# Low weight parts of the convolution stage by an adding DMA instead of VectorE

## The chip, the cores and the metric

The kernel runs on one core of a Trainium2 chip. The metric is the device time of one execution in microseconds (us). Before the change three runs took 1458.36, 1458.60 and 1459.15 us; the median is 1458.6 us. Five engines work beside each other and are tied by semaphores: TensorE (PE in the rows; PEld is its weight load), VectorE (DVE), ScalarE (ACT), GpSimd (POOL) and SyncE (SP), which only issues DMAs here.

## The reference, cut to what matters

Two transformer blocks on 512 tokens of 1024 features, float32. The part around the change is the mixer of the second block:

```
def conformer_conv(x, w_in, b_in, conv_w, conv_b, ln_g, ln_b, w_out, b_out):
    a, g = jnp.split(x @ w_in + b_in, 2, axis=-1)
    h = a * jax.nn.sigmoid(g)
    h = lax.conv_general_dilated(h, conv_w[:, None, :], window_strides=(1,),
        padding=[(CONV_KERNEL - 1, 0)], ..., feature_group_count=D_MODEL) + conv_b
    h = jax.nn.silu(layer_norm(h, ln_g, ln_b))
    return h @ w_out + b_out
```

`CONV_KERNEL` is 31: every feature is convolved over time with its own 31 taps. `x @ w_in` is 1024 to 2048 features, `h @ w_out` 1024 to 1024.

## The kernel before, in words

**Dense layers.** Every weight matrix is cut into units of 128 output features (128 partitions x 1024 float32, 512 KB). A unit passes through four stages, in four slots (`SLOTS`): SP loads it into `raw`; ScalarE copies it to `whi`, which rounds it to the type float32r (`split_hi`, L891, semaphore `hi_done`); VectorE subtracts, `wlo = raw - whi` (`split_lo`, L1273, semaphore `lo_done`); TensorE multiplies eight tiles, three products for each (`whi*xh`, `whi*xl`, `wlo*xh`, L543 to L545). One unit is a chain of 24 matmuls into one PSUM bank. SP waits for `lo_done` of the unit that used the slot before; ScalarE waits for `chain_done` of that unit.

**The convolution stage.** It works on eight chunks c = 0 to 7 of 128 features. Chunk c needs two units of `w_ain`, 2c (gate) and 2c+1 (value). TensorE runs, for each c, the chains of units 2c and 2c+1, then `convolve(c-1)`, then `statistics(c-3)`. The 31 taps of a chunk are divided among the engines by three tables:

- `PE_TAPS`: taps on TensorE, as matmuls with diagonal weights, two taps to a pair (L817); ScalarE makes the diagonals (L1176).
- `POOL_TAPS`: ScalarE multiplies (`tapped`, L1190, a ring of 9 buffers), GpSimd adds (L532). n taps are n - 1 additions.
- `LATE_TAPS`: VectorE, after `convolve`, in the same PSUM bank (L1632).
- What is left are VectorE's own taps (L1619, L1622). A chunk that has some needs one more addition in `collect` (L1640).

The order on each engine is written out by hand. VectorE in chunk c: evict and gate the value unit (L1653, L1663, which gives `hc`), then own taps of c and late taps of c - 1 in turn, with the two `split_lo` of units 2c+3 and 2c+4 and the eviction of unit 2c+2 at fixed places among them, then `collect(c-1)` (L1640, L1645). ScalarE in chunk c: products, then `split_hi` of unit 2c+5, the sigmoid of the next chunk, the diagonals, `split_hi` of unit 2c+6. GpSimd in chunk c only adds. `hc` is copied in shifted form to `shifted` by four DMAs before `convolve` may start. Units 16 to 23 in this count are those of `w_aout`, of which TensorE begins three at once after the layer norm.

Of the kernel before, what the change touches and what calls it, by code (L numbers as in the profile page):

```python
# [22 lines left out]
F32 = mybir.dt.float32  # L23
F32R = mybir.dt.float32r
ALU = mybir.AluOpType
# [6 lines left out]
C = D // P  # L32
# [7 lines left out]
FF_PARTS = (8, 8, 6)  # L40
MLP_PARTS = (8, 8, 8, 8)
TAPS = 31
PE_TAPS = (8, 6, 6, 8, 8, 8, 14, 22)
SHIFTS = 2
GROUP = P // SHIFTS
GATE_AT = 8
DIAGS = 3
POOL_TAPS = (11, 11, 11, 11, 11, 10, 9, 5)
LATE_TAPS = (0, 6, 10, 12, 12, 13, 8, 0)
LATE_START = (2, 2, 2, 0, 0, 0, 0, 4)  # L50
PARTS = 9
LAST_DIAGS = 5
HC = 3
SLOTS = 4
AHEAD = 3
WARM = 10
# [104 lines left out]
def build(nc, xT, vec_in, cst_in, w_in, out):  # L161
# [3 lines left out]
    with ExitStack() as ctx:  # L165
# [76 lines left out]
        w_loaded = [sem(f"w_loaded{s}") for s in range(SLOTS)]  # L242
        hi_done = sem("hi_done")
        lo_done = sem("lo_done")
        chain_done = sem("chain_done")
        acc_free = sem("acc_free")
        setup = sem("setup")
# [130 lines left out]
        def used(unit):  # L378

            return 2 * unit + 2 if isinstance(unit, int) and unit < 4 else unit + 5  # L380

        def loads(base, i, k):

            return 16 * (i + (base + k) // SLOTS + 1)

# [4 lines left out]
        def _(sp):  # L390

            def load(p, i, k):
                unit = p.unit + SLOTS * i + k
                if isinstance(unit, int) and unit < SLOTS:
                    free, at = None, unit - p.unit
                elif isinstance(i, int):
                    free, at = unit - SLOTS + 1, SLOTS * i + k
                else:
                    free, at = sp.snap(unit - SLOTS + 1), sp.snap(SLOTS * i + k)
                if p.name == "ain":  # L400
                    at = at ^ 1
                src = p.weights[at] if isinstance(at, int) else \
                    p.weights[bass.ds(at, 1)].rearrange("o p n -> p (o n)")
                if free is not None:
                    sp.wait_ge(lo_done, free)
                sp.dma_start(raw[:, k, 0:p.tiles * P], src).then_inc(w_loaded[k], 16)

# [69 lines left out]
        @block.gpsimd  # L477
        def _(pool):


            pool.wait_ge(setup, 1)
            pool.wait_ge(cst_loaded, 16)
            for g in range(2):
                pool.wait_ge(squared, 2 * g + 2)
                nc.gpsimd.tensor_tensor(square_of(2 * g), square_of(2 * g), square_of(2 * g + 1), ALU.add)\
                    .then_inc(early_summed, 1)
            pool.wait_ge(early_summed, 2)
            nc.gpsimd.tensor_tensor(square_of(0), square_of(0), square_of(2), ALU.add).then_inc(early_summed, 1)
            nc.gpsimd.tensor_copy(near[:, 0, PAD:PAD + P], ident).then_inc(near_steps, 1)
            for g in range(4):  # L490
                pool.wait_ge(near_steps, g + 2)
                nc.gpsimd.tensor_tensor(near[:, g + 1, on], near[:, g, on],
                                        near[:, g, PAD - (1 << g):2 * PAD + P - (1 << g)], ALU.add)\
                    .then_inc(near_steps, 1)

            def add_squares(name):

                per = 2 if name == "ain" else 1
                for n in range(per * C):
                    which = n % 2 if name == "ain" else 0  # L500
                    x = (prod if name == "ain" and n // 2 % 2 else sq)[:, n % 2, :]
                    pool.wait_ge(sq_ready, SQ[name] + n + 1)
                    pool.wait_ge(ssum_ready, SS[name] + n + 1)
                    nc.gpsimd.tensor_tensor(ssum[:, which, :], ssum[:, which, :], x, ALU.add)\  # L504
                        .then_inc(ssum_ready, 1)

            add_squares("ffn0")
            add_squares("qkv")
            for s in range(len(STEPS)):
                k0 = P if STEPS[s][1] == 0 else 0  # L510
                pool.wait_ge(den_steps, 2 * s + 2)
                a = prob[:, s % 3, :, k0:2 * P]
                nc.gpsimd.tensor_tensor(a, a, stat[:, 5, s, :].rearrange("p (i o) -> p i o", o=1)
                                        .broadcast_to([P, REP, 2 * P - k0]), ALU.mult).then_inc(p_scaled, 1)
            for m in range(2 * C):
                at = slice(m // C * 2 * P, (m // C + 1) * 2 * P)
                pool.wait_ge(sq_ready, SQ["ffn1"] + m + 1)
                pool.wait_ge(ssum_ready, SS["ffn1"] + m + 1)
                nc.gpsimd.tensor_tensor(ssum[:, 0, at], ssum[:, 0, at], sq[:, m % 2, at], ALU.add)\
                    .then_inc(ssum_ready, 1)  # L520
            add_squares("ain")

            made = adds = 0
            for c in range(C):
                if c >= 2:
                    pool.wait_ge(hv_ready, c - 1)
                for k in range(1, POOL_TAPS[c]):
                    a = tapped[:, made % PARTS, :] if k == 1 else prod[:, c % 2, :]
                    pool.wait_ge(tapped_ready, made + k + 1)
                    if k > 1:  # L530
                        pool.wait_ge(tapped_steps, adds)
                    nc.gpsimd.tensor_tensor(prod[:, c % 2, :], a, tapped[:, (made + k) % PARTS, :], ALU.add)\  # L532
                        .then_inc(tapped_steps, 1)
                    adds += 1
                made += POOL_TAPS[c]
            add_squares("mlp")
# [3 lines left out]
        def _(pe):  # L540
# [6 lines left out]
            def chain(p, i, k, hi, lo):  # L547

                chain_no = p.chain + SLOTS * i + k
                pe.wait_ge(lo_done, p.unit + SLOTS * i + k + 1)  # L550
                pe.wait_ge(acc_free, chain_no - 3)
                for t in range(p.tiles):
                    w = slice(t * P, (t + 1) * P)
# [4 lines left out]
            def first_chains(name, norm_name, n=2):  # L558

                p = ph[name]  # L560
                pe.wait_ge(lo_done, p.unit + n)
                pe.wait_ge(acc_free, p.chain + n - 4)
                for t in range(C):
                    if t == C - 2 and norm_name != "ffn0":
# [298 lines left out]
                                          start=True, stop=True)  # L863
                mm.then_inc(spread_done, 1)
            fill(LN_FILL[2])
            pe.wait_ge(lo_done, p.unit + LN_UNITS)
            for t in range(C):
                pe.wait_ge(ln_lo, t + 1)
                w = slice(t * P, (t + 1) * P)
# [12 lines left out]
        def _(act):  # L882
# [309 lines left out]
                                         bias=v("conv_b", c) if k == 0 else 0.0).then_inc(tapped_ready, 1)  # L1192

            nc.scalar.activation(eps[:, 3:4], eps[:, 0:1], ACT.Sqrt)
            def square(c):

                act.wait_ge(hv_ready, c + 1)
# [19 lines left out]
            for c in range(C):  # L1217
# [12 lines left out]
                if c < C - 1:  # L1230
                    if c < C - 2:
                        split_hi(p.unit, 0, 2 * c + 2 + AHEAD)
                        sigmoid(c + 1)
                    if c + 1 == C - 1:
                        diagonals(c + 1, 1, 2)
                    else:
                        diagonals(c + 1)
                    if c < C - 2:
                        split_hi(p.unit, 0, 2 * c + 3 + AHEAD)
                else:  # L1240
                    split_hi(p.unit, 0, 2 * c + AHEAD)
                    split_hi(p.unit, 0, 2 * c + 1 + AHEAD)
# [21 lines left out]
        def _(dve):  # L1264
# [402 lines left out]
            for c in range(C):  # L1667
# [21 lines left out]
                gate_at = next((n for n in range(rounds) if issued[n] >= GATE_AT), rounds - 1)  # L1689
                for n in range(rounds):  # L1690
                    for j in range(2):
                        if n == split_at[j] and c < C - 1 and (c or j):
                            split_lo(p.unit, 0, 2 * c + j + AHEAD)
                    if n == gate_at and c < C - 1:
                        evict(c + 1, 0)
# [138 lines left out]
```

## Time and profile before

| | before |
|---|---|
| median of 3 runs | 1458.6 us |
| profiled execution, its own time | 1457.93 us |
| its span, first to last instruction | 1456.1 us |
| PE, PEld busy | 1442.8, 1174.9 us |
| DVE, ACT, POOL busy | 929.2, 631.2, 210.9 us |
| granted TensorE clock, mean | 1.00 of full speed (2.4 GHz) |

The profile was taken from one execution, whose own time stands beside its span: 1.8 us lie outside the span. Times in the rows count from the span's start. The convolution stage runs from about 914 us (first matmul of unit 0) to about 1049 us (last statistics). A busy PE is not PE at its peak, since matmuls overlap: starts of neighbouring matmuls are more telling than busy time.

### The profile page before, as it was taken

How to read it: one execution, taken by the hardware profiler on the slowest of the kernel's cores; microseconds unless marked ns; L12 is line 12 of the kernel's file. 1: busy time of each engine (PE TensorE's matmuls, PEld its weight loads, DVE VectorE, ACT ScalarE, POOL GpSimd, SP SyncE). 2: the span in 40 equal slices, each digit the busy share in tenths (PEclk: the TensorE clock that was granted, in tenths of full speed). 3: DMA queues.
4: the chain of work that ended last, by engine and by line, in shares of the span. 5: the costliest groups of instructions: out<-in, count | busy, mean ns of one | idle time of the engine just before them, and what ended most of it. 6: DMA issues, size and time to landing. Idle time of an engine off the chain costs nothing.

```text
span 1456.1 us, 19997 instructions
## 1 busy us (share of the span) xinstructions
PE 1442.8 (99%) x6852; PEld 1174.9 (81%) x6852; DVE 929.2 (64%) x1330; ACT 631.2 (43%) x999; POOL 210.9 (14%) x155
## 2 busy tenths in 40 slices
PE   9999999999999999999999999999999999999999
PEld 8788888888877898888888888766578888888887
DVE  7877773573645667767754756899998653544532
ACT  7444442342546665444432425777754322222210
POOL 4000000000302241000000004599611000000000
PEclk9999999999999999999999999999999999999999
DMA  5233233232422012332332333243313333232321
GB/s 191 86 101 101 88 103 113 78 104 81 131 81 69 30 60 87 101 102 87 101 116 72 102 96 92 87 130 88 102 33 105 111 102 99 90 104 95 102 94 50
DMA packets 42397, 137.01 MB, mean 94 GB/s; under 512 B 4960, under 2 KB 5984, under 8 KB 42336
## 3 DMA queue, kind: packets, MB, share of 16 engines
q1 hardware_dynamic: 41200, 133.80, 28.5%
q10 hardware_dynamic: 1136, 2.42, 0.4%
q8 instruction: 35, 0.57, 0.2%
q14 instruction: 26, 0.21, 0.0%
HBM read 129.85 MB, written 2.10 MB: 91 GB/s over the span
## 4 chain that ended last, share of the span: by engine, by line
PE 85%; POOL 7%; DVE 4%; ACT 2%; issue 1%; DMA 0%; ACTq 0%; POOLq 0%; DVEq 0%
PE bank L543 27%; PE bank L545 27%; PE bank L544 27%; POOL prod L532 6%; PE bank L691 1%; PE bank L719 1%; PE bank L704 1%; DVE bank L1622 1%; DMA cst<-cst_in 0%; DVE wlo L1273 0%; PE bank L584 0%; DVE hv L1746 0%; ACT res L1025 0%; DVE ylo L1712 0%; ACT whi L891 0%
## 5 line engine op out<-in xcount | busy, mean ns | idle before, releaser
L543 PE MATMUL bank<-xh,whi 128*128 128x512 f32 x1184 | 465.2, 393 | 1.5 <-DVE res L1561 0.7
L545 PE MATMUL bank<-xh,wlo 128*128 128x512 f32 x1184 | 461.2, 390 | 0.0
L544 PE MATMUL bank<-xl,whi 128*128 128x512 f32 x1184 | 461.0, 389 | 0.0
L891 ACT ACTIVATE whi<-raw 128x1024 fp32r<-128x1024 f32 x244 | 255.6, 1050 | 235.1 <-PE bank L545 233.8
L1273 DVE TENSOR_TENSOR wlo<-raw,whi 128x1024 fp32r<-128x1024 f32 x244 | 312.4, 1281 | 43.6 <-ACT whi L891 35.5
L543 PEld LDWEIGHTS bank<-xh,whi 128*128 128x128 f32 x1184 | 222.3, 188 | 55.8 <-issue 7.1
L544 PEld LDWEIGHTS bank<-xl,whi 128*128 128x128 f32 x1184 | 222.4, 188 | 46.7 <-issue 1.2
L545 PEld LDWEIGHTS bank<-xh,wlo 128*128 128x128 f32 x1184 | 222.3, 188 | 46.6
L543 PE MATMUL bank<-ahi,whi 128*128 128x512 f32 x608 | 236.7, 389 | 0.0
L544 PE MATMUL bank<-alo,whi 128*128 128x512 f32 x608 | 236.7, 389 | 0.0
L545 PE MATMUL bank<-ahi,wlo 128*128 128x512 f32 x608 | 236.6, 389 | 0.0
L1294 DVE TENSOR_TENSOR res<-bank,res 128x512 f32 (+1 forms) x80 | 55.2, 690 | 202.6 <-PE bank L545 202.6
L504 POOL TENSOR_TENSOR ssum<-ssum,sq 128x512 f32<-128x512 f32 x32 | 47.8, 1494 | 738.6 <-ACT sq L911 407.0
L1345 DVE SCALAR_TENSOR_TENSOR tmp<-u,vec,tmp 128x512 f32<-128x512 f32 x176 | 124.2, 747 | 31.8 <-ACT tmp L950 31.8
L544 PEld LDWEIGHTS bank<-alo,whi 128*128 128x128 f32 x608 | 114.2, 188 | 23.7
L545 PEld LDWEIGHTS bank<-ahi,wlo 128*128 128x128 f32 x608 | 114.2, 188 | 23.7
L543 PEld LDWEIGHTS bank<-ahi,whi 128*128 128x128 f32 x608 | 114.2, 188 | 23.6
L950 ACT ACTIVATE tmp<-u,vec 128x512 f32<-128x512 f32 x88 | 71.6, 814 | 125.3 <-DVE u L1340 125.3
L1340 DVE TENSOR_TENSOR u<-bank,rinv 128x512 f32<-128x512 f32 x88 | 59.4, 685 | 63.9 <-PE bank L545 63.9
L532 POOL TENSOR_TENSOR prod<-prod,tapped 128x512 f32<-128x512 f32 x63 | 92.9, 1475 | 9.3 <-POOL prod L532 0.4
L972 ACT ACTIVATE ahi<-tmp 128x512 f32 (+1 forms) x32 | 20.2, 632 | 121.8 <-DVE tmp L1370 121.8
L954 ACT ACTIVATE gate<-tmp 128x512 f32<-128x512 f32 x44 | 27.9, 633 | 96.2 <-DVE tmp L1345 96.2
(183 smaller groups left out, 1315.6 us busy)
## 6 DMA issues: line engine op xcount, KB each, us to landing
raw<-w_ffn_up SPq DMA_DIRECT2D x88, 512.0 KB, 3.4
raw<-w_ffn_down SPq DMA_DIRECT2D x32, 512.0 KB, 3.4
raw<-w_mlp_up SPq DMA_DIRECT2D x32, 512.0 KB, 3.3
raw<-w_mlp_down SPq DMA_DIRECT2D x32, 512.0 KB, 3.3
raw<-w_ain SPq DMA_DIRECT2D x16, 512.0 KB, 3.3
raw<-w_ffn_down SPq DMA_DIRECT2D x16, 384.0 KB, 3.1
raw<-w_qkv SPq DMA_DIRECT2D x12, 512.0 KB, 3.4
raw<-w_wo SPq DMA_DIRECT2D x8, 512.0 KB, 3.5
```

Source lines behind the costliest of these rows:

```text
L504: nc.gpsimd.tensor_tensor(ssum[:, which, :], ssum[:, which, :], x, ALU.add)\
L532: nc.gpsimd.tensor_tensor(prod[:, c % 2, :], a, tapped[:, (made + k) % PARTS, :], ALU.add)\
L543: nc.tensor.matmul(out_, hi, mh, start=first, stop=False)
L544: nc.tensor.matmul(out_, hi, ml, start=False, stop=False)
L545: return nc.tensor.matmul(out_, lo, mh, start=False, stop=last)
L891: nc.scalar.activation(whi[:, s, 0:tiles * P], raw[:, s, 0:tiles * P], ACT.Copy)\
L950: nc.scalar.activation(tmp[:, k, :], u[:, k, 2:2 + T], ACT.Identity, scale=col(vec, par + 2), bias=col(vec, par + 3))\
L954: nc.scalar.activation(gate[:, b, :], tmp[:, 2 * b + 1, :], ACT.Silu)\
L1273: V.tensor_tensor(wlo[:, s, 0:tiles * P], raw[:, s, 0:tiles * P], whi[:, s, 0:tiles * P].bitcast(F32), ALU.subtract).then_inc(lo_done, 1)
L1294: V.tensor_tensor(row(res, c), acc[k][:], row(res, c), ALU.add).then_inc(acc_free, 1)
L1340: V.tensor_tensor(u[:, k, 2:2 + T], acc[k][:], rinv[:], ALU.mult).then_inc(acc_free, 1)
L1345: V.scalar_tensor_tensor(tmp[:, k, :], u[:, k, shift:shift + T], col(vec, par + 4 * j + shift), tmp[:, k, :], op0=ALU.mult, op1=ALU.add).t ...
```

## The change

For units 5 to 16 of the stage (`ADDED`; 11 of `w_ain`, one of `w_aout`) the low part is made in another way. ScalarE writes `wlo = -whi` (`negate_high`), GpSimd then issues a DMA that reads the same weights from HBM again and adds them into `wlo`. GpSimd issues the two DMAs of units 2c+3 and 2c+4 ahead of its additions of chunk c. TensorE waits for that DMA (`low_added`) where it waited for `lo_done`; SP may refill `raw` as soon as `hi_done` is reached. VectorE's subtractions for these units go.

The tap tables change: TensorE has two taps fewer in chunks 3 and 4; GpSimd's additions go from 10, 10, 10, 10, 10, 9, 8, 4 to 10, 9, 8, 8, 8, 8, 7, 4; late taps are 60 instead of 61; VectorE's own taps go from 12, 8, 4, 0, 0, 0, 0, 4 to 12, 10, 7, 4, 3, 2, 0, 4, so that chunks 3, 4 and 5 need the additional `L1640`.

```diff
-PE_TAPS = (8, 6, 6, 8, 8, 8, 14, 22)
+PE_TAPS = (8, 6, 6, 6, 6, 8, 14, 22)
-POOL_TAPS = (11, 11, 11, 11, 11, 10, 9, 5)
-LATE_TAPS = (0, 6, 10, 12, 12, 13, 8, 0)
+POOL_TAPS = (11, 10, 9, 9, 9, 9, 8, 5)
+LATE_TAPS = (0, 5, 9, 12, 13, 12, 9, 0)
+ADDED = tuple(range(5, 17))
...
+        def low_parts(unit):
+
+            if isinstance(unit, int):
+                return unit + 1 - sum(ph["ain"].unit + e <= unit for e in ADDED)
+            return unit + 1
...
+        def wait_low(eng, unit, passed=0):
+
+            if is_added(unit):
+                eng.wait_ge(low_added[unit % SLOTS], 16 * added_in_slot(unit))
+            else:
+                eng.wait_ge(lo_done, low_parts(unit) - (0 if isinstance(unit, int) else passed))
...
-                if free is not None:
+                if is_added(unit - SLOTS):
+                    sp.wait_ge(hi_done, unit - SLOTS + 1)
+                elif free is not None:
                     sp.wait_ge(lo_done, free)
...
             for c in range(C):
+                for e in (2 * c + AHEAD, 2 * c + AHEAD + 1):
+                    if e in ADDED:
+                        pool.wait_ge(low_negated, ADDED.index(e) + 1)
+                        weights = ph["ain"].weights[e ^ 1] if e < 2 * C else ph["aout"].weights[e - 2 * C]
+                        nc.gpsimd.dma_start(wlo[:, e % SLOTS, :], weights, accum_op=ALU.add)\
+                            .then_inc(low_added[e % SLOTS], 16)
                 if c >= 2:
                     pool.wait_ge(hv_ready, c - 1)
...
             def chain(p, i, k, hi, lo):
 
                 chain_no = p.chain + SLOTS * i + k
-                pe.wait_ge(lo_done, p.unit + SLOTS * i + k + 1)
+                wait_low(pe, p.unit + SLOTS * i + k, passed(p))
...
+            def negate_high(e):
+
+                act.wait_ge(hi_done, p.unit + e + 1)
+                nc.scalar.activation(wlo[:, e % SLOTS, :], whi[:, e % SLOTS, :].bitcast(F32), ACT.Copy, scale=-1.0)\
+                    .then_inc(low_negated, 1)
+
...
                     if c < C - 2:
                         split_hi(p.unit, 0, 2 * c + 2 + AHEAD)
                         sigmoid(c + 1)
+                        negate_high(2 * c + 2 + AHEAD)
...
                     if c < C - 2:
                         split_hi(p.unit, 0, 2 * c + 3 + AHEAD)
+                        negate_high(2 * c + 3 + AHEAD)
...
-                        if n == split_at[j] and c < C - 1 and (c or j):
+                        if n == split_at[j] and c == 0 and j:
                             split_lo(p.unit, 0, 2 * c + j + AHEAD)
```

GpSimd, from its additions of chunk 0 on, before (L532 is an addition, `x9` nine alike; one pair of rows is one chunk):

```order
L532 TENSOR_TENSOR prod<-tapped 128x512
L532 TENSOR_TENSOR prod<-prod,tapped 128x512 x9
L532 TENSOR_TENSOR prod<-tapped 128x512
L532 TENSOR_TENSOR prod<-prod,tapped 128x512 x9
L532 TENSOR_TENSOR prod<-tapped 128x512
L532 TENSOR_TENSOR prod<-prod,tapped 128x512 x9
```

The same place after the change (L568 is the addition, L559 the adding DMA):

```order
L568 TENSOR_TENSOR prod<-tapped 128x512
L568 TENSOR_TENSOR prod<-prod,tapped 128x512 x9
L559 DMA wlo<-w_ain 128x1024 x2
L568 TENSOR_TENSOR prod<-tapped 128x512
L568 TENSOR_TENSOR prod<-prod,tapped 128x512 x8
L559 DMA wlo<-w_ain 128x1024 x2
L568 TENSOR_TENSOR prod<-tapped 128x512
L568 TENSOR_TENSOR prod<-prod,tapped 128x512 x7
```

The DMAs of units 5 and 6 stand behind all ten additions of chunk 0, those of units 7 and 8 behind chunk 1.

VectorE in chunk 1, from the value unit's gate on, before (L1273 is the subtraction for units 5 and 6, L1622 an own tap, L1653 an eviction):

```order
L1663 SCALAR_TENSOR_TENSOR hc<-bank,vec,gate 128x512
L1619 TENSOR_SCALAR bank<-hc,vec 128x512
L1273 TENSOR_TENSOR wlo<-raw,whi 128x1024
L1622 SCALAR_TENSOR_TENSOR bank<-hc,vec,bank 128x512 x4
L1273 TENSOR_TENSOR wlo<-raw,whi 128x1024
L1622 SCALAR_TENSOR_TENSOR bank<-hc,vec,bank 128x512 x2
L1653 TENSOR_TENSOR tmp<-bank,rinv 128x512
L1622 SCALAR_TENSOR_TENSOR hv<-hc,vec,bank 128x512
L1640 TENSOR_TENSOR hv<-prod,hv 128x512
L1645 TENSOR_TENSOR hv<-bank,hv 128x512
```

The same place after:

```order
L1709 SCALAR_TENSOR_TENSOR hc<-bank,vec,gate 128x512
L1665 TENSOR_SCALAR bank<-hc,vec 128x512
L1668 SCALAR_TENSOR_TENSOR bank<-hc,vec,bank 128x512 x7
L1699 TENSOR_TENSOR tmp<-bank,rinv 128x512
L1668 SCALAR_TENSOR_TENSOR bank<-hc,vec,bank 128x512
L1668 SCALAR_TENSOR_TENSOR hv<-hc,vec,bank 128x512
L1686 TENSOR_TENSOR hv<-prod,hv 128x512
L1691 TENSOR_TENSOR hv<-bank,hv 128x512
```

Two subtractions are gone and two own taps have come; the rest keeps its order.

## Rows read from the trace of the kernel before

**Rows 1.** The page's chain that ended last, shares of the whole span by line.
```profile
PE bank L543 27%; PE bank L545 27%; PE bank L544 27%; POOL prod L532 6%; PE bank L691 1%; PE bank L719 1%; PE bank L704 1%; DVE bank L1622 1%; DMA cst<-cst_in 0%; DVE wlo L1273 0%; PE bank L584 0%; DVE hv L1746 0%; ACT res L1025 0%; DVE ylo L1712 0%; ACT whi L891 0%
```

**Rows 2.** Busy time by stretch: window, length, PE, PEld, DVE, ACT, POOL, PEclk, DMA, GB/s.
```profile
950.00:970.00 20.00, 20.00 (x89) 12.83 (x87) 19.65 (x25) 15.08 (x26) 18.42 (x13) 1.00 0.39 116
1030.00:1049.00 19.00, 17.45 (x80) 5.87 (x76) 17.97 (x25) 14.35 (x29) 14.55 (x12) 1.00 0.12 30
```

**Rows 3.** Timeline of TensorE: start, us, engine, line, operation, tiles, count.
```profile
937.80 3.65 PE L817 MATMUL bank<-shifted,dg 128*64 128x512 f32 x16
...
947.11 0.50 PE L543 MATMUL bank<-xh,whi 128*128 128x512 f32 x1
...
952.81 2.80 PE L817 MATMUL bank<-shifted,dg 128*64 128x512 f32 x12
955.54 0.49 PE L543 MATMUL bank<-xh,whi 128*128 128x512 f32 x1
...
961.13 0.39 PE L543 MATMUL bank<-xh,whi 128*128 128x512 f32 x1
...
970.24 0.50 PE L543 MATMUL bank<-xh,whi 128*128 128x512 f32 x1
...
985.79 0.50 PE L543 MATMUL bank<-xh,whi 128*128 128x512 f32 x1
...
1028.01 0.65 PE L817 MATMUL bank<-shifted,dg 128*64 128x512 f32 x2
...
1036.05 0.65 PE L817 MATMUL bank<-shifted,dg 128*64 128x512 f32 x2 [0.96 <-DVE hv L1645]
```

**Rows 4.** Timeline of GpSimd in the convolution stage.
```profile
933.80 1.29 POOL L532 TENSOR_TENSOR prod<-tapped 128x512 f32<-128x512 f32 x1 [13.44 <-ACT tapped L1190]
...
949.59 1.30 POOL L532 TENSOR_TENSOR prod<-tapped 128x512 f32<-128x512 f32 x1
...
1029.31 1.27 POOL L532 TENSOR_TENSOR prod<-tapped 128x512 f32<-128x512 f32 x1
...
1040.47 1.27 POOL L532 TENSOR_TENSOR prod<-tapped 128x512 f32<-128x512 f32 x1
```

**Rows 5.** The chain of waits in order of time: start, us, what.
```profile
946.07 2.14 POOL prod L532
```

**Rows 6.** Timeline of VectorE: unit 5's subtraction, and the stage's end.
```profile
945.84 1.22 DVE L1273 TENSOR_TENSOR wlo<-raw,whi 128x1024 fp32r<-128x1024 f32 x1
...
1028.94 0.68 DVE L1653 TENSOR_TENSOR tmp<-bank,rinv 128x512 f32<-128x512 f32 x1
1029.54 0.69 DVE L1653 TENSOR_TENSOR bank<-bank,rinv 128x512 f32<-128x512 f32 x1
1030.41 0.75 DVE L1663 SCALAR_TENSOR_TENSOR hc<-bank,vec,gate 128x512 f32<-128x512 f32 x1 [0.18 <-ACT gate L1205]
```

**Rows 7.** Timeline of ScalarE ahead of chunk 1's products.
```profile
945.17 2.04 ACT L1190 ACTIVATE tapped<-hc,vec 128x512 f32<-128x512 f32 x3 [1.58 <-DVE hc L1663]
```

**Rows 8.** Groups from 930 to 1048 us: busy, mean ns of one, idle before.
```profile
L1632 DVE SCALAR_TENSOR_TENSOR bank<-hc,vec,bank 128x512 f32<-128x512 f32 x61 | 46.0, 753 | 1.6
...
L1273 DVE TENSOR_TENSOR wlo<-raw,whi 128x1024 fp32r<-128x1024 f32 x14 | 24.8, 1773 | 0.0
...
L891 ACT ACTIVATE whi<-raw 128x1024 fp32r<-128x1024 f32 x16 | 16.5, 1043 | 0.0
...
L1640 DVE TENSOR_TENSOR hv<-prod,hv 128x512 f32<-128x512 f32 x4 | 3.9, 977 | 0.1
```

**Rows 9.** GpSimd's 128x1024 operation, from its groups over the whole span.
```profile
L513 POOL TENSOR_TENSOR prob<-prob,stat 128x1024 f32<-128x1024 f32 (+1 forms) x16 | 26.9, 1680 | 106.9 <-DVE stat L1538 106.9
```

**Rows 10.** Issues of SyncE, start and us of the group.
```profile
932.26 2.44 SPq L439 DMA_DIRECT2D shifted<-hc  x4
```

**Rows 11.** DMA issues of the whole span: count, KB each, us to landing.
```profile
raw<-w_ain SPq DMA_DIRECT2D x16, 512.0 KB, 3.3
...
res<-xT ACTq DMA_DIRECT2D x3, 512.0 KB, 8.1
```

More of the change, by code:

```diff
@@ L244, in build @@
         lo_done = sem("lo_done")
+        low_negated = sem("low_negated")
+        low_added = [sem(f"low_added{s}") for s in range(SLOTS)]
         chain_done = sem("chain_done")
@@ L380, in used, with is_added, added_in_slot, passed @@
             return 2 * unit + 2 if isinstance(unit, int) and unit < 4 else unit + 5
+        def is_added(unit):
+            return isinstance(unit, int) and unit - ph["ain"].unit in ADDED
+        def low_parts(unit):
+            if isinstance(unit, int):
+                return unit + 1 - sum(ph["ain"].unit + e <= unit for e in ADDED)
+            return unit + 1
+        def added_in_slot(unit):
+            return sum(is_added(e) for e in range(unit % SLOTS, unit + 1, SLOTS))
+        def wait_low(eng, unit, passed=0):
[3 more added lines that the diff above has]
+                eng.wait_ge(lo_done, low_parts(unit) - (0 if isinstance(unit, int) else passed))
+        def passed(p):
+            return len(ADDED) if p.unit > ph["aout"].unit else 0
         def loads(base, i, k):
@@ L396, in load @@
                 elif isinstance(i, int):
-                    free, at = unit - SLOTS + 1, SLOTS * i + k
+                    free, at = low_parts(unit - SLOTS), SLOTS * i + k
                 else:
-                    free, at = sp.snap(unit - SLOTS + 1), sp.snap(SLOTS * i + k)
+                    free, at = sp.snap(unit - SLOTS + 1 - passed(p)), sp.snap(SLOTS * i + k)
                 if p.name == "ain":
@@ L560, in first_chains @@
                 p = ph[name]
-                pe.wait_ge(lo_done, p.unit + n)
+                wait_low(pe, p.unit + n - 1)
                 pe.wait_ge(acc_free, p.chain + n - 4)
@@ L865, in _ @@
             fill(LN_FILL[2])
-            pe.wait_ge(lo_done, p.unit + LN_UNITS)
+            for k in range(LN_UNITS):
+                wait_low(pe, p.unit + k)
             for t in range(C):
```

## Prediction

> **What bounds the kernel now.** Read the page's chain first. Three lines of TensorE hold 81% of the span, each 27%, and GpSimd's additions 6% [rows 1]. 6% of 1456.1 us is 87 us, and these additions exist only in the convolution stage: read alone, the chain says that GpSimd bounds this stage, and that nine additions fewer are a gain.
>
> The busy times by stretch speak against it: from 950 to 970 us TensorE is busy all the time, VectorE 19.65 of 20 us, GpSimd 18.42, ScalarE 15.08 [rows 2]. Three engines are full, so the gaps must be looked for in TensorE's starts. Unit 5's first matmul stands at 947.11; after 24 matmuls the pairs of taps follow at 952.81, unit 6 at 955.54, unit 7 at 961.13, so a unit takes about 5.6 us. Unit 8 begins at 970.24, unit 10 at 985.79 [rows 3]. Eight taps take 3.65 us and six take 2.80 [rows 3], so a pair costs 0.85. From unit 6 to unit 8 are 14.7 us with six taps, from 8 to 10 15.55 with eight: the difference is that one pair. So TensorE runs without holes worth naming until 1028.01, when unit 15 has ended; the only wait up to the last convolution is that before 1036.05 [rows 3]. TensorE sets the stage's pace, GpSimd and VectorE are nearly as slow, and whatever makes TensorE wait is paid in full: there is no later slack in which it could catch up.
>
> The second fact that matters: unit 5's low part is just in time. VectorE begins it at 945.84 and takes 1.22 us [rows 6], so it ends at 947.06; TensorE starts the unit at 947.11 [rows 3].
>
> **The change part by part.**
>
> *TensorE.* Two pairs of taps go, both ahead of unit 15: 2 x 0.85 = 1.7 us gained.
>
> *Unit 5's low part.* It now stands on GpSimd's queue behind the ten additions of chunk 0. These began at 933.80 and chunk 1's began at 949.59 [rows 4]. One of them, at 946.07, took 2.14 us [rows 5] while VectorE did unit 5's subtraction. Unhindered additions are 1.40 apart: 1029.31 to 1040.47 are eight [rows 4]. 2.14 and the 0.1 between two of them less 1.40 is 0.84, which goes with the subtraction. GpSimd is free at 949.59 - 0.84 = 948.75. That alone is 1.65 us later than TensorE wants the finished part. Then come the issue (d) and the landing (l).
>
> No row shows a DMA issued by GpSimd. For d the nearest rows are SyncE's issues, 2.44 us for four, 0.6 each [rows 10], and GpSimd's own slowest operation, 1.68 us for 128x1024 [rows 9]. I take 1.0, between the two and nearer to the issue. For l a plain load of the same 512 KB lands in 3.3 us, and the slowest loads of this size, those from the start, in 8.1 [rows 11]. The adding DMA must read what it adds to as well, so I take 5.0, one and a half loads. Should the queue let an issue start under the last addition, 1.4 us come back; that is the end below. Stall of unit 5: 1.65 + 1.0 + 5.0 = 7.7 us; at the ends 1.65 - 1.4 + 0 + 3.3 = 3.6 and 1.65 + 1.7 + 8.1 = 11.4.
>
> The Trainium skill (DMA: Bandwidth & Descriptors, section "Anatomy of one DMA — SWDGE (gpsimd) path") puts such a DMA at about 2.0 us and the bytes at 436 GB/s, which would be an estimate of 3.2 us for 512 KB. By it the stall would be about 5.9 us with the same d; it says nothing of an added operand, and no run here shows it yet.
>
> *Unit 7's low part* stands behind the two issues and the nine additions of chunk 1: 2d + 9 x 1.40 + 0.3, the last for the L1640 that VectorE lays beside them, 977 ns [rows 8] against 0.69 us for an eviction of the same size [rows 6]. That is 12.9 + 2d after unit 5's. TensorE needs it 961.13 - 947.11 = 14.0 us after unit 5 [rows 3]. So unit 7 adds 2d - 1.1 = 0.9 us of stall (nothing for d under 0.55, 2.3 for d = 1.7).
>
> *Units 9 to 15.* The interval on GpSimd is 2d + 8 x 1.40 + 0.3 = 13.5 us, TensorE's is 14.7: no more stalls below d = 1.6. The even units are issued with the odd ones and needed 5.6 to 9 us after them.
>
> *VectorE.* Eleven of the stage's subtractions go at 1.77 us, and that of unit 16; they come back as 13 taps more (14 own, one late less) at 0.75 and three L1640 at 0.98 [rows 8]: about -21.2 + 9.8 + 2.9 = -8.5 us. In chunk 4, with 15 taps, three evictions and gates of 0.7 and two collecting operations, it is 15 x 0.78 + 2.1 + 1.7 = 15.5 us, close to TensorE's 14.7: what it loses there it can take from the stall before. None of this shortens the stage, since VectorE waits for TensorE's delayed chains.
>
> *ScalarE.* Twelve negations at about 1.04, like the copy L891 [rows 8], less nine products and four diagonals, are some 5 us more over eight chunks. It is busy 15.08 of 20 us [rows 2]. At chunk 1 the two negations (2.1 us) meet an idle time of 1.58 us [rows 7] and push the products by 0.5, which GpSimd, busy until 948.75, does not feel. Nothing on the path. If this cover went, one negation would cost 1.04.
>
> *SyncE* waits for `hi_done`, which comes earlier, so loads and the shifted copies behind them are never later. The 512 KB read again per unit are inside l. In the last MLP TensorE computes one more register per chain; it has 24 matmuls of time for it: nothing.
>
> *The stage's end.* Before, unit 15 ended with 1028.01, but VectorE evicted unit 14 only at 1028.94 and gated at 1030.41 [rows 3, 6]. Now VectorE stands ready when unit 15 ends, so unit 15 to `hc` shrinks by about 1.7 us. The path behind is longer by one L1640, 1.0. Net -0.7.
>
> *Clock.* Every stretch shows 1.00 [rows 2], and TensorE never idles for so long as here. If the granted clock falls in the stall, part of unit 5 runs at 1.2 GHz; the whole unit would cost 5.6 us more, none of it nothing. I take 1.5, nearer to zero since no row shows a fall.
>
> *Sum:* 7.7 + 0.9 - 1.7 - 0.7 + 1.5 = +7.7 us. On the profiled execution's own 1457.93 us that is 1465.6; it lies 0.7 below the median, so 1466.3. The ends: 3.6 + 0 - 1.7 - 0.7 + 0 = +1.2 and 11.4 + 2.3 - 1.7 - 0.7 + 5.6 = +16.9, to 1475.5.
>
> **The rivals.**
>
> *A, it is faster.* GpSimd is the bound, as the chain has it [rows 1]: nine additions (12.6 us) and some eight blocks of 0.84 (6.7) go, twelve issues of d = 1.0 come, 7 us fewer. TensorE's work caps that: 1.7 for the pairs and at most 1.2 of the wait at the end, 2.9 us, to 1455.7. For it: the chain. Against it: TensorE's starts. It decides only if unit 5's DMA lands within 2.9 us of 947.1, hence by 950.0, only 1.25 us after GpSimd is free, less than any transfer in the trace takes. 3%.
>
> *B, no change.* The stall stays below 5.3 us (l near 3.3, d at 0.4 or less). Net below 2.9 us: within 1461.5. 9%.
>
> *C, GpSimd becomes the bound.* With d = 3 each interval is 17.5 against 14.7: 1.65 + 3 + 5 for unit 5, 4.9 at unit 7, four times 2.8, less 2.4: +23 us, 1482. For it: descriptors made in software are no short work. 8%.
>
> *D, the clock.* TensorE stands still for 7.7 us, and the restarted unit runs entirely at 1.2 GHz: 5.6 instead of 1.5, 1470.4. Against it: no row shows the lower level. 12%. The Trainium skill (TensorE: Matmul & The Clock Gate, section "Part 1: The HAM clock gate") says that idleness halves the clock until sustained work restores it; in this trace nothing contradicts it, nothing shows it.
>
> **How the numbers follow.** The forecast, a stall at unit 5 of 5.3 to 11.4 us that is never made good, has 68%, its own range 1461.5 to 1472. With B above its middle, D and part of C, 1461 to 1475 holds 8 in 10: left out are A, the lower half of B and most of C. A measurement here tells 0.2%, 2.9 us, from no change. Faster is A, 3%; same is B, 9%; slower is the rest, 88%.
>
> **What would show it.** In the changed profile: unit 5's first matmul at 954 to 955 us, its wait named as the DMA of `wlo`; a second, smaller wait at unit 7; none at 9 to 15, with 14.7 us between units 8, 10 and 12; VectorE waiting for unit 15; the last statistics 6 to 8 us later than now; everything before 945 and after the layer norm of unchanged length. The forecast is wrong if unit 5 starts before 950 us, if the wait there is short and waits are spread over all odd units (C), or if a sum of TensorE's waits above 5 us does not show in the span.

## The result, and the profile after

The changed kernel takes 1467.5 us (median of 6 runs, 1466.3 to 1467.8) against 1458.7 us (median of 6, 1458.4 to 1459.2) before: a ratio of 1.0059, 95% interval 1.0046 to 1.0072. It is slower, by 8.85 us; 7.7 were forecast. The profiled execution took 1467.84 us, its span is 1466.0 us.

The chain that ended last, shares by line, the row that answers to [rows 1]:

```profile
PE bank L579 29%; PE bank L580 28%; PE bank L581 28%; PE bank L853 2%; PE bank L727 1%; PE bank L755 1%; POOL prod L568 1%; PE bank L740 1%; DMA wlo<-w_ain 1%; DMA res<-xT 0%; PE bank L863 0%; PE bank L620 0%; ACT whi L928 0%; DVE hv L1792 0%; DVE wlo L1319 0%
```

GpSimd's additions fell from 6% to 1%, and the kernel became slower. Their place in the chain before had said nothing of what removing them brings. New is `DMA wlo<-w_ain`, 1%, which is some 10 us at one single place. TensorE's timeline around that place and on to the end of the stage (L579 to L581 are the three products, L853 the pairs of taps, L863 the statistics), to be read against [rows 3]:

```profile
947.42 0.39 PE L581 MATMUL bank<-xh,wlo 128*128 128x512 f32 x1
957.29 0.79 PE L579 MATMUL bank<-xh,whi 128*128 128x512 f32 x1 [9.49 <-DMA wlo<-w_ain]
...
961.30 0.63 PE L579 MATMUL bank<-xh,whi 128*128 128x512 f32 x1
962.58 0.63 PE L579 MATMUL bank<-xh,whi 128*128 128x512 f32 x1
...
964.22 0.40 PE L579 MATMUL bank<-xh,whi 128*128 128x512 f32 x1
964.92 0.39 PE L579 MATMUL bank<-xh,whi 128*128 128x512 f32 x1
965.70 2.80 PE L853 MATMUL bank<-shifted,dg 128*64 128x512 f32 x12
...
979.54 2.80 PE L853 MATMUL bank<-shifted,dg 128*64 128x512 f32 x12
994.23 2.80 PE L853 MATMUL bank<-shifted,dg 128*64 128x512 f32 x12
1008.92 2.80 PE L853 MATMUL bank<-shifted,dg 128*64 128x512 f32 x12
1023.60 3.65 PE L853 MATMUL bank<-shifted,dg 128*64 128x512 f32 x16
1039.16 6.23 PE L853 MATMUL bank<-shifted,dg 128*64 128x512 f32 x28
1046.07 9.61 PE L853 MATMUL bank<-shifted,dg 128*64 128x512 f32 x44
```

Unit 5 waits 9.49 us. When it runs, three matmuls take 1.28 us (961.30 to 962.58), later 0.70 (964.22 to 964.92). The unit takes 965.70 - 957.29 = 8.41 us; before it took 952.81 - 947.11 = 5.70 [rows 3]. The clock column by stretch (after the window: its length, PE, PEld, DVE, ACT, POOL, PEclk, DMA share, GB/s), against 1.00 in both stretches of [rows 2]:

```profile
945.00:950.00 5.00, 2.81 (x13) 1.99 (x11) 4.71 (x7) 4.97 (x8) 4.57 (x5) 1.00 0.50 120
950.00:955.00 5.00, 0.00 (x0) 0.00 (x0) 4.86 (x8) 4.29 (x8) 4.71 (x5) 0.79 0.91 240
955.00:960.00 5.00, 2.71 (x6) 2.15 (x7) 0.53 (x1) 4.31 (x9) 4.57 (x4) 0.50 0.84 165
960.00:965.00 5.00, 5.00 (x17) 3.94 (x16) 0.00 (x0) 0.00 (x0) 4.57 (x6) 0.69 0.00 0
965.00:970.00 5.00, 5.00 (x23) 2.39 (x22) 3.99 (x6) 2.60 (x5) 2.18 (x3) 1.00 0.86 147
```

The granted clock fell to 0.50 (1.2 GHz) while TensorE stood still and came back between 960 and 965 us. From 955 to 965 VectorE is almost empty: it waits for TensorE's late chains (10.28 us until 965.80), which is where its relief of 8 us went.

GpSimd, the rows that answer to [rows 4], and the landings (KB each, median us from issue to landing) from 930 to 1060 us, to be read against the 3.3 us in [rows 11]:

```profile
935.93 13.55 POOL L568 TENSOR_TENSOR prod<-prod,tapped 128x512 f32<-128x512 f32 x9
949.41 1.91 POOL L559 DMA_DIRECT2D wlo<-w_ain  x2
950.69 1.92 POOL L568 TENSOR_TENSOR prod<-tapped 128x512 f32<-128x512 f32 x1
...
964.39 1.76 POOL L559 DMA_DIRECT2D wlo<-w_ain  x2
968.97 1.29 POOL L568 TENSOR_TENSOR prod<-tapped 128x512 f32<-128x512 f32 x1 [2.82 <-ACT tapped L1227]
```

```profile
wlo<-w_ain POOLq DMA_DIRECT2D x11, 512.0 KB, 7.8
raw<-w_ain SPq DMA_DIRECT2D x9, 512.0 KB, 5.9
...
shifted<-hc SPq DMA_DIRECT2D x16, 129.0 KB, 5.7
```

SyncE's loads of `raw` beside the first adding DMA, after, and the same two loads before:

```profile
948.30 1.07 SPq L436 DMA_DIRECT2D raw<-w_ain  x2
```

```profile
947.61 4.72 SPq L406 DMA_DIRECT2D raw<-w_ain  x2
```

The second of the two was issued at 952.00 before. Since SyncE now waits for `hi_done` it goes out at 948.93, so that two loads are under way when GpSimd issues the adding DMAs of units 5 and 6.

The account, as the start of the same work after less its start before:

| work | before | after | shift |
|---|---|---|---|
| first matmul of the first dense layer | 30.95 | 31.63 | 0.68 |
| unit 5 | 947.11 | 957.29 | 10.18 |
| pairs of taps behind unit 5 | 952.81 | 965.70 | 12.89 |
| pairs of chunk 2 (behind unit 7) | 966.66 | 979.54 | 12.88 |
| pairs of chunk 6 (behind unit 15) | 1028.01 | 1039.16 | 11.15 |
| pairs of chunk 7 | 1036.05 | 1046.07 | 10.02 |
| last group of statistics | 1048.25 | 1058.23 | 9.98 |

So: 0.7 from the start of this execution (a scatter of the start, long before any changed instruction), 9.5 of stall, 2.7 of clock, nothing at unit 7, -1.7 for the two pairs, -1.2 at the stage's end; together 10.0, and the span grew by 9.9. Without the scatter of the start it is 9.3.

### The profile page after: what moved, and what is told of

Read it like the earlier page. It is cut to its first block, busy times and chain, and to the rows that moved or that the text cites. A ratio compares the mean times of both kernels' runs of the same rounds, so it can differ in the third digit from the quotient of the medians.

```text
span 1466.0 us, 19979 instructions
## 1 busy us (share of the span) xinstructions
PE 1444.0 (98%) x6844; PEld 1175.5 (80%) x6844; DVE 921.5 (63%) x1334; ACT 635.4 (43%) x998; POOL 199.9 (14%) x158
## 4 chain that ended last, share of the span: by engine, by line
PE 91%; DVE 3%; ACT 2%; POOL 1%; issue 1%; DMA 1%; ACTq 0%; POOLq 0%; DVEq 0%
PE bank L579 29%; PE bank L580 28%; PE bank L581 28%; PE bank L853 2%; PE bank L727 1%; PE bank L755 1%; POOL prod L568 1%; PE bank L740 1%; DMA wlo<-w_ain 1%; DMA res<-xT 0%; PE bank L863 0%; PE bank L620 0%; ACT whi L928 0%; DVE hv L1792 0%; DVE wlo L1319 0%
## 5 line engine op out<-in xcount | busy, mean ns | idle before, releaser
L579 PE MATMUL bank<-xh,whi 128*128 128x512 f32 x1184 | 466.2, 394 | 11.0 <-DMA wlo<-w_ain 9.5
L581 PE MATMUL bank<-xh,wlo 128*128 128x512 f32 x1184 | 461.9, 390 | 0.0
L1319 DVE TENSOR_TENSOR wlo<-raw,whi 128x1024 fp32r<-128x1024 f32 x232 | 290.3, 1252 | 43.1 <-ACT whi L928 35.1
L579 PEld LDWEIGHTS bank<-xh,whi 128*128 128x128 f32 x1184 | 222.9, 188 | 65.9 <-DMA wlo<-w_ain 9.9
L581 PEld LDWEIGHTS bank<-xh,wlo 128*128 128x128 f32 x1184 | 222.9, 188 | 46.7
L579 PE MATMUL bank<-ahi,whi 128*128 128x512 f32 x608 | 236.5, 389 | 0.0
L581 PE MATMUL bank<-ahi,wlo 128*128 128x512 f32 x608 | 236.5, 389 | 0.0
L579 PEld LDWEIGHTS bank<-ahi,whi 128*128 128x128 f32 x608 | 114.1, 188 | 23.7
L581 PEld LDWEIGHTS bank<-ahi,wlo 128*128 128x128 f32 x608 | 114.1, 188 | 23.7
L568 POOL TENSOR_TENSOR prod<-prod,tapped 128x512 f32<-128x512 f32 x54 | 71.3, 1320 | 8.0 <-POOL prod L568 0.4
```

Of the source, the lines that this page charges most:

```text
L579: nc.tensor.matmul(out_, hi, mh, start=first, stop=False)
L581: return nc.tensor.matmul(out_, lo, mh, start=False, stop=last)
L1319: V.tensor_tensor(wlo[:, s, 0:tiles * P], raw[:, s, 0:tiles * P], whi[:, s, 0:tiles * P].bitcast(F32), ALU.subtract).then_inc(lo_done, 1)
```

## The experiments

All ratios are to the kernel before, run on the same chip beside them, with their 95% interval. Runs 2, 4 and 5 shorten `ADDED`; for the units that drop out, their edits also leave out the negation and put the subtraction on VectorE back at its place of before.

**1. Fill the stall.** 34 small matmuls of ones on ones ahead of the wait.

```diff
+FILL_5 = 34
...
+                if p.name == "ain" and SLOTS * i + k == 5:
+                    pe.wait_ge(acc_free, chain_no - 3)
+                    for _ in range(FILL_5):
+                        nc.tensor.matmul(acc[k][:, 0:P], ones[:], ones[:], start=True, stop=True)
```

> The changed kernel, with 34 small matmuls (ones on ones, into the accumulator that the unit overwrites) that TensorE runs just ahead of its wait for unit 5's low part. They fill the stall and do nothing else. If the clock is a term of its own, the granted clock stays at 1.00 through unit 5, the unit takes 5.7 us instead of 8.4, and the time falls by about 2.7 us against the changed kernel: a ratio to before of 1.004 instead of 1.006. The stall itself stays (first matmul of unit 5 near 957). Rival: the slow records after the stall are another thing (low parts or activations still being written, memory contention with the landing DMA): then unit 5 stays at 8.4 us and the time stays at 1.006, or grows where the filling outlasts the stall.

Measured: 1465.7 us, ratio 1.0050 (1.0033 to 1.0067). TensorE:

```profile
956.64 0.50 PE L580 MATMUL bank<-xh,whi 128*128 128x512 f32 x1 [1.84 <-DMA wlo<-w_ain]
...
962.33 2.80 PE L858 MATMUL bank<-shifted,dg 128*64 128x512 f32 x12
```

```profile
955.00:960.00 5.00, 3.35 (x15) 2.76 (x16) 0.00 (x0) 3.76 (x9) 4.43 (x5) 1.00 0.71 139
```

The unit starts as late as ever but takes 5.69 us, at a clock of 1.00, with the same transfers beside it. So the 2.7 us went with the clock, and not with contention. The medians differ by only 1.8 us (a ratio of 1.004 was expected), the spans of the two profiled executions by 3.3; the unit itself says 2.7. The four executions are not alike: two at a mean clock of 1.000 took 1464.55 and 1465.05 us, two at 0.999 took 1466.39 and 1467.31. That the filling held the clock only in the first two is likely but not shown, since the profile is of one execution.

**2. Begin with unit 7.** Units 5 and 6 are subtracted on VectorE again.

```diff
-ADDED = tuple(range(5, 17))
+ADDED = tuple(range(7, 17))
```

> The changed kernel, but units 5 and 6 have their low parts subtracted on VectorE as before; the adding DMA begins with unit 7. Theory: the stall comes from where the first DMA stands, behind a chunk's additions and so one chunk too late, and not from unit 5 itself. Then unit 5 starts at 947 to 948, the stall moves to unit 7, whose DMA is issued near 963 while TensorE wants it at 961.8: it lands at about 970 to 971, 8 to 9.5 us late, and the time is 1.004 to 1.007 of before, like the changed kernel. Rival: the first DMAs on this queue are slow because they are the first, or because of the loads in flight at unit 5 only: then unit 7 waits less than 5 us and the ratio is below 1.003.

Measured: 1468.4 us, ratio 1.0067 (1.0050 to 1.0083). GpSimd's first issue, and TensorE's unit 7:

```profile
963.41 1.91 POOL L559 DMA_DIRECT2D wlo<-w_ain  x2
```

```profile
971.65 0.80 PE L579 MATMUL bank<-xh,whi 128*128 128x512 f32 x1 [10.30 <-DMA wlo<-w_ain]
...
979.07 2.37 PE L853 MATMUL bank<-shifted,dg 128*64 128x512 f32 x10
```

Unit 5 starts in time, at 947.17, and the stall moves to unit 7, 10.3 us long, with 1.9 us of clock behind it (the unit takes 7.42 us instead of 5.53). So the stall is not bound to unit 5: the first unit whose DMA stands behind a chunk's additions pays, once, and after it TensorE is late enough for all others. The rival is not wholly out, though. That first DMA landed in 8.2 us, those of the later odd units in 5.2 to 5.5, and again two loads had been issued just ahead of it:

```profile
962.67 1.07 SPq L436 DMA_DIRECT2D raw<-w_ain  x2
```

**3. Plain DMAs.** The same transfers at the same places, without adding. The subtraction is left out with it: the low part becomes the whole weight, so the output is another one, and only the times count.

```diff
-                        nc.gpsimd.dma_start(wlo[:, e % SLOTS, :], weights, accum_op=ALU.add)\
+                        nc.gpsimd.dma_start(wlo[:, e % SLOTS, :], weights)\
```

> The changed kernel, with GpSimd's DMAs plain instead of adding: what they leave in the low part is the whole weight and not the weight less its high part, so this kernel computes something else. Position and size of the transfers are the same. If adding is what makes the landing long (7.8 us in the median, against 3.3 for a plain load issued by SyncE), the landing falls to 3.5 to 5 us, the stall at unit 5 shrinks by 3 to 4 us, and the ratio to before falls to about 1.003. If it is the software queue or two pairs of 512 KB loads at once that make it long, the landing stays above 7 us and the ratio at 1.006.

Measured: 1465.4 us, ratio 1.0044 (1.0028 to 1.0061).

```profile
955.33 0.80 PE L579 MATMUL bank<-xh,whi 128*128 128x512 f32 x1 [7.44 <-DMA wlo<-w_ain]
```

```profile
wlo<-w_ain POOLq DMA_DIRECT2D x11, 512.0 KB, 4.9
```

The median landing falls from 7.8 to 4.9 us. At unit 5 it counts less: issued at 949.49, used at 955.33, 5.8 us, against 957.29 - 949.41 = 7.9 with adding. Leaving out the adding takes 2.0 us off there, less than the 3 to 4 expected, and the ratio stays above the 1.003 expected.

**4. One adding DMA at a time.** Only the odd units.

```diff
-ADDED = tuple(range(5, 17))
+ADDED = (5, 7, 9, 11, 13, 15)
```

> The changed kernel, but only the odd units get an adding DMA; the even ones are subtracted on VectorE as before. So one adding DMA is in flight at a time instead of two. If the landing of 7.8 us comes from the two sharing the queue, unit 5's falls to 4.5 to 6 us and the unit starts at 953.5 to 955.5 instead of 957; if adding itself is slow, or the loads beside it slow it, the landing stays above 6.5 us and the start within 1 us of 957. The time of the whole tells less: VectorE has five subtractions of 1.77 us back that it has no room for in the later chunks, so 1.004 to 1.010 of before.

Measured: 1465.8 us, ratio 1.0047 (1.0032 to 1.0062).

```profile
949.90 1.00 POOL L559 DMA_DIRECT2D wlo<-w_ain  x1
```

```profile
955.81 0.79 PE L579 MATMUL bank<-xh,whi 128*128 128x512 f32 x1 [7.52 <-DMA wlo<-w_ain]
```

From issue to use 5.9 us instead of 7.9, and the median landing is 5.8. That looks like the price of the second adding DMA, but the run took away more than that: with unit 6 subtracted on VectorE its slot comes free later, and the second load of `raw` is issued at 953.32 instead of 948.93. In the changed kernel the DMAs of units 7, 9, 11, 13 and 15 landed in 5.5, 5.5, 5.3, 5.0 and 5.2 us, four of them with a second adding DMA 0.6 to 0.7 us behind, and none with a load under way at its issue. A second adding DMA alone therefore does not lengthen the first; at unit 5 the loads ahead of it are the likelier cause, which no run tried by itself. Runs 3 and 4 each take 2 us off at unit 5, and what both together would take is not known. Even so the least stall was 7.4 us, since some 1.6 us stand ahead of the issue.

**5. Only the taps.** No adding DMA; VectorE subtracts as before.

```diff
-ADDED = tuple(range(5, 17))
+ADDED = ()
```

> Only the taps move, as in the changed kernel; all low parts are subtracted on VectorE as before, and GpSimd issues no DMA. Theory (VectorE has no room for 13 taps more unless the subtractions go): unit 5 is in time, TensorE's clock stays at 1.00, but VectorE needs 13 x 0.78 + 3 x 0.98 = 13 us more in chunks 1 to 6, of which it has some 2 in idle time; the low parts and activations come late, TensorE waits in the later chunks, and the time is 6 to 11 us above before (1.004 to 1.008). Rival: VectorE has slack that the busy shares do not show, and the two pairs of taps are a gain by themselves: 0.999 of before.

Measured: 1464.9 us, ratio 1.0039 (1.0024 to 1.0055).

```profile
964.08 0.50 PE L579 MATMUL bank<-xh,whi 128*128 128x512 f32 x1 [1.85 <-DVE wlo L1321]
...
971.35 2.80 PE L853 MATMUL bank<-shifted,dg 128*64 128x512 f32 x12
```

```profile
965.00:970.00 5.00, 5.00 (x17) 3.98 (x17) 5.00 (x7) 3.33 (x5) 4.71 (x4) 0.71 0.36 111
```

As the theory had it, VectorE cannot carry the taps and the subtractions: units 7 and 13 wait 1.9 us each for it, and the 6.0 us lost are at the low end of the 6 to 11 expected. But the waits are only 3.8 us. The clock, which was expected to stay at 1.00, fell behind each of them: unit 7 took 7.27 us instead of the 5.53 of before (961.13 to 966.66), unit 13 7.25, another 3.5 us together. The two pairs take 1.7 off again.

**6. Only the DMAs,** with the taps of before.

```diff
-PE_TAPS = (8, 6, 6, 6, 6, 8, 14, 22)
+PE_TAPS = (8, 6, 6, 8, 8, 8, 14, 22)
-POOL_TAPS = (11, 10, 9, 9, 9, 9, 8, 5)
-LATE_TAPS = (0, 5, 9, 12, 13, 12, 9, 0)
+POOL_TAPS = (11, 11, 11, 11, 11, 10, 9, 5)
+LATE_TAPS = (0, 6, 10, 12, 12, 13, 8, 0)
```

> Only the adding DMAs, as in the changed kernel, with the taps of before (TensorE's two pairs and GpSimd's nine additions stay). Theory: the stall at unit 5 and the slow records after it are as in the changed kernel (start near 957, 8.4 us for the unit: 12 us). GpSimd's interval is 10 x 1.40 + 1.8 + 0.3 = 16.1 us against TensorE's 14.7 to 15.6, so that odd units from 7 to 15 may wait again, up to 1 us each, but the loads hidden in the stall give some of it back; the pairs do not come off. Time 1.008 to 1.011 of before. Rival: the stall is all there is and GpSimd's additions are free: 1.007, the changed kernel and its 1.7 us of pairs.

Measured: 1472.7 us, ratio 1.0093 (1.0077 to 1.0108).

```profile
956.95 0.80 PE L579 MATMUL bank<-xh,whi 128*128 128x512 f32 x1 [9.48 <-DMA wlo<-w_ain]
...
992.32 0.50 PE L579 MATMUL bank<-xh,whi 128*128 128x512 f32 x1 [3.85 <-DMA wlo<-w_ain]
```

The stall is the same, and unit 9 waits 3.85 us more: not a little at each odd unit, as expected, but once. Two things meet there. With ten additions GpSimd does fall behind, as in the forecast's rival C: it issues unit 9's DMA at 983.00, 2.35 us later than in the changed kernel. And two loads of `raw`, issued 0.3 and 0.9 us behind it, go beside it: it lands in 9.3 us instead of 5.5, which is 3.8 of the wait. The fewer additions of the change kept this away, but GpSimd's pace alone would hardly have made a wait (an estimate: 983.00 + 5.5 = 988.5, and TensorE was ready at 988.47).

**7. Issue earlier.** GpSimd issues the same DMAs between the additions of the chunk before (ahead of the fourth for the odd unit, ahead of the eighth for the even one, as the trace has it; the expectation below counts one more); ScalarE makes that odd unit's two parts in the middle of its products, and the even unit's ahead of the diagonals.

```diff
+ISSUE_AT = (4, 8)
+SPLIT_EARLY = 4
...
+                    for e, at in ((2 * c + 2 + AHEAD, ISSUE_AT[0]), (2 * c + 3 + AHEAD, ISSUE_AT[1])):
+                        if k == at and e in ADDED:
+                            add_weights(e)
...
-                products(c, range(2, LAST_DIAGS))
+                products(c, range(2, SPLIT_EARLY if c < C - 2 else LAST_DIAGS))
+                if c < C - 2:
+                    split_hi(p.unit, 0, 2 * c + 2 + AHEAD)
+                    negate_high(2 * c + 2 + AHEAD)
+                    products(c, range(SPLIT_EARLY, LAST_DIAGS))
```

> The changed kernel with the same work at another place: ScalarE makes the high part and its negative for the odd unit of the next chunk in the middle of its products, and GpSimd issues that unit's adding DMA after four of the chunk's additions and the even unit's after eight, instead of both behind all of them. Theory (the stall is the DMA's place on GpSimd's queue): the DMA of unit 5 is issued near 940 and has landed by 948 to 949, the wait at unit 5 is below 2 us, TensorE's clock stays at 1.00, and the two pairs of taps remain as a gain: 1455 to 1458 us, a ratio of 0.998 to 1.000. Rival 1: the landing is bound by something that comes later (the raw load, the negation on ScalarE, which now delays the products): unit 5 waits 3 us or more, ratio 1.002 and above. Rival 2: the adding DMAs cost by their traffic (loads and copies between buffers land late everywhere): then waits appear at other units, with unit 5 in time.

Measured: 1455.8 us, ratio 0.9981 (0.9972 to 0.9991). GpSimd's first issue and TensorE's longest wait in the stage:

```profile
938.89 1.01 POOL L559 DMA_DIRECT2D wlo<-w_ain  x1
939.64 5.90 POOL L574 TENSOR_TENSOR prod<-prod,tapped 128x512 f32<-128x512 f32 x4
```

```profile
953.33 2.80 PE L859 MATMUL bank<-shifted,dg 128*64 128x512 f32 x12 [0.58 <-DMA shifted<-hc]
```

Nothing waits for an adding DMA any more, and the clock is 1.00. Unit 5's DMA takes 6.2 us to land, but from 938.89, and is there at 945.11. The 12 us of stall and clock are gone with the earlier place, on GpSimd and on ScalarE that feeds it. So the cause is the place: landings of 5.2 to 7.7 us cost nothing once they start early enough. What remains of rival 2 is 0.58 us: the copies of `hc` land later beside the new traffic.

**8. Earlier, with the taps of before.** Run 7 with the tables of run 6's diff.

> The version with the DMAs issued between the additions of the chunk before, with the taps of before: 10 additions a chunk on GpSimd, eight PE taps in chunks 3 to 5, VectorE rid of the subtractions and of nothing else. Theory (the 2.9 us that the early version gains are TensorE's two pairs and the shorter end of the stage): unit 5 is in time, and the two pairs do not come off; GpSimd's interval is 10 x 1.44 + 1.5 = 15.9 us, about what it was before (16.0 to 16.4), so its parts stay in time: 1457.5 to 1459.0 us, 0.999 to 1.000 of before. Rival: GpSimd falls behind with twelve issues more, its DMAs come too late for the odd units from 9 on, and TensorE waits there as in the run with the old taps: 1.002 or more.

Measured: 1459.5 us, ratio 1.0004 (0.9995 to 1.0013).

```profile
978.38 0.50 PE L585 MATMUL bank<-xh,whi 128*128 128x512 f32 x1 [1.12 <-DMA wlo<-w_ain]
...
1010.70 0.50 PE L585 MATMUL bank<-xh,whi 128*128 128x512 f32 x1 [0.50 <-DMA wlo<-w_ain]
```

No change to before; the median lies just above the 1457.5 to 1459.0 expected, and its rival is right in small: GpSimd falls a little behind, and units 9 and 13 wait. The two parts of the change need each other: the DMAs alone buy nothing even in the right place, the taps alone cost 6 us, both together and in the right place gain 2.9.

**9. One more pair off TensorE** in chunk 5, on top of run 7.

```diff
-PE_TAPS = (8, 6, 6, 6, 6, 8, 14, 22)
+PE_TAPS = (8, 6, 6, 6, 6, 6, 14, 22)
-LATE_TAPS = (0, 5, 9, 12, 13, 12, 9, 0)
+LATE_TAPS = (0, 5, 9, 12, 13, 13, 9, 0)
```

> The version with the DMAs issued between the additions of the chunk before, and one more pair of taps of chunk 5 moved from TensorE to VectorE, which waits 4.5 us for TensorE there. If TensorE is the only bound of that chunk, unit 15 ends 0.85 us earlier and so does the kernel: 1455.0 us, a ratio to before of 0.9975. Rival: VectorE sets the end of the stage (its late taps of chunk 6 end together with TensorE's last convolution), and its two taps more (1.55 us) are paid partly there: 1455.8 or more, no gain.

Measured: 1456.0 us, ratio 0.9980 (0.9971 to 0.9989), no gain over run 7: the rival is right. VectorE's last taps:

```profile
1036.55 7.08 DVE L1685 SCALAR_TENSOR_TENSOR bank<-hc,vec,bank 128x512 f32<-128x512 f32 x9
1043.73 0.69 DVE L1698 TENSOR_TENSOR hv<-bank,prod 128x512 f32<-128x512 f32 x1
```

The last convolution had started at 1033.75 and taken 9.6 us, so TensorE was done at 1043.4 while VectorE still had three operations of 0.7 us ahead of it.

**10. And a pair back to TensorE** in chunk 6, for two of VectorE's late taps.

```diff
-PE_TAPS = (8, 6, 6, 6, 6, 6, 14, 22)
-LATE_TAPS = (0, 5, 9, 12, 13, 13, 9, 0)
+PE_TAPS = (8, 6, 6, 6, 6, 6, 16, 22)
+LATE_TAPS = (0, 5, 9, 12, 13, 13, 7, 0)
```

> The version with the DMAs issued between the additions of the chunk before; one pair of chunk 5's taps goes from TensorE to VectorE, as in the last run, and two of VectorE's late taps of chunk 6 come back to TensorE as a pair. The last run showed that VectorE sets the end of the stage when it gets two taps more. If so, unit 15 ends 0.85 us earlier, VectorE's last late tap ends 1.5 us earlier than in the last run, TensorE's last convolution (0.85 us more ahead of it) ends as in the early version or 0.7 us sooner: 1455.1 to 1455.8 us, 0.9975 to 0.998 of before. Rival: the end hangs on the chain from hc of the last chunk over its shifted copies and its 44 matmuls, which only the 0.85 us of unit 15 shorten, and the pair given back takes them again: no gain over the early version, 1455.9 or more.

Measured: 1454.7 us, ratio 0.9972 (0.9961 to 0.9982), 4.4 us below the kernel before, the best of all and 0.4 us better than the expected range.

```profile
1041.05 0.69 DVE L1698 TENSOR_TENSOR hv<-bank,prod 128x512 f32<-128x512 f32 x1
1041.66 0.68 DVE L1693 TENSOR_TENSOR hv<-prod,hv 128x512 f32<-128x512 f32 x1
1043.12 0.69 DVE L1698 TENSOR_TENSOR hv<-bank,hv 128x512 f32<-128x512 f32 x1 [0.79 <-PE bank L859]
```

VectorE now waits 0.79 us for TensorE's last convolution, where in run 9 TensorE's statistics had waited for what VectorE delivered.

## Why the prediction was right, and where it was not

*TensorE bounds the stage, and its waits are never made good.* Right, against the chain's hint at GpSimd: 12.9 us of shift behind unit 5 are still 12.9 at chunk 2, and only the two pairs and the stage's end take anything off.

*When GpSimd is free.* 948.75 forecast; measured 949.41, or 948.73 without the start's 0.68. The nine additions took 13.55 us instead of 14.40, so the 0.84 us that went with VectorE's subtraction did come off.

*Issue and landing.* d = 1.0 and l = 5.0 forecast, 6.0 together. From the start of the issue to the matmul the trace has 957.29 - 949.41 = 7.9. The issue was 1.0, as taken; the landing is the term that was mis-sized, by 2 us. Counted alike it is more: the landings of [rows 11] run from the start of the issue and hold it already, so d was added to l once too often, and 5.0 stood against 7.8. "One and a half loads" was nevertheless a fair size for the transfer: the later odd units landed in 5.0 to 5.5 us. What failed is that it was taken as good at unit 5. The forecast had seen that SyncE's loads come earlier and booked it as harmless ("never later"); but two of them, of 512 KB each, were issued 1.1 and 0.5 us ahead of the adding DMA, where before they had been 4.4 us apart. Wherever the first adding DMA had two such loads ahead it took 7.8 to 8.2 us (this kernel, runs 1, 2 and 6), and 5.9 where there was one (run 4). That the loads are the reason is argued from these times; no run moved the loads alone. Run 3 shows that without adding the same place would have cost 5.8. The estimate of 3.2 us from the Trainium skill (DMA: Bandwidth & Descriptors, section "Anatomy of one DMA — SWDGE (gpsimd) path") is far below the 5.0 to 9.6 us of the adding DMAs here; even plain transfers took 4.9 in the median, beside other traffic.

*Unit 7.* 0.9 us forecast, nothing measured. The interval on GpSimd is 964.39 - 949.41 = 15.0 us, against 14.9 forecast, but by two errors that cancel: the two issues held GpSimd for 1.3 us and not 2.0, the nine additions took 13.7 and not 12.9. The wait did not come for two reasons. The forecast took the same landing for both units, and unit 7's was 5.5 us and not 7.8. And it counted the slow clock and the wait at unit 7 side by side, though every us that unit 5 takes longer leaves unit 7's DMA one more. The clock is not needed for it: in run 1, at full clock, unit 7 does not wait either, its landing being 6.6 us.

*Units 9 to 15.* No waits, 14.7 us between the pairs of chunks 2, 3, 4 and 5, as forecast.

*The pairs.* -1.7 forecast; 12.88 - 11.15 = 1.73 measured.

*The stage's end.* -0.7 forecast, -1.2 measured (9.98 - 11.15). VectorE stood waiting for unit 15 (3.8 us), as said, and TensorE's 0.96 us of wait there is gone.

*Clock.* 1.5 taken in a range of 0 to 5.6, 2.7 measured: between the forecast and rival D. The trace agrees in kind with the Trainium skill (TensorE: Matmul & The Clock Gate, section "Part 1: The HAM clock gate"), that idleness halves the clock until sustained work restores it: 0.50 in the stall, 1.00 again before unit 5 had ended.

*VectorE, ScalarE.* VectorE's busy time fell by 7.7 us (8.5 forecast), ScalarE's grew by 4.2 (some 5 forecast), both without effect on the path.

The stall at unit 5 and the clock were both sized too small, by 1.8 and 1.2 us, unit 7 and the end too dear, by 0.9 and 0.5: 9.3 us instead of 7.7 in this trace, 8.85 in the medians. The total came as near as it did because these errors partly cancel. For the same reason unit 5 began at 957.3 and not at 954 to 955, and the last statistics came 9.3 us later (without the start's 0.68) and not 6 to 8.

## What to carry to other kernels

When work goes from a full engine to a DMA queue, the first question is not what the transfer costs but what stands ahead of its issue in the program's order: here the same twelve DMAs cost 12 us behind ten additions and 0.6 us between them. The second is what else is under way when it is issued, since a semaphore that comes earlier can move other transfers on top of it. A stall of TensorE is to be priced with the slow matmuls behind it. And a rebalancing pays only when its parts come together, so it is worth trying the position before giving up the idea.

## What the runs showed of the hardware

- An adding DMA of 512 KB issued by GpSimd, the first of a pair, landed 5.0 to 5.5 us after the start of its issue at units 7 to 15 of the changed kernel, and in 7.8 us at unit 5, where two loads had been issued within 1.1 us ahead (8.2 at unit 7 in run 2, where it was the same). The second of a pair took 8.4 to 9.6. The first of two plain ones took 5.8 at unit 5 (run 3).
- A single adding issue is a row of 0.86 to 1.0 us on GpSimd, but the next addition began 0.6 to 0.75 us after its start; two issues held GpSimd for 1.3 us. Two plain ones were rows of 1.25 and 1.10 us.
- The extra traffic is felt by others: loads of `raw` landed in 5.9 us instead of 3.4, half of the copies of `hc` in 5.7 instead of 2.4 (medians of the stage).
- Waits far shorter than the one of the change lowered TensorE's clock. Behind 1.85 us (run 5, granted clock 0.50 from 965 to 966 us) and 3.85 us (run 6, 0.74 from 992 to 995, the unit took 7.30 us) the unit that followed ran partly at 1.2 GHz and cost another 1.7 us; behind 1.12 us (run 8) the clock stayed at 1.00 and the unit took 5.70.
